# Both MLP products of a decoder layer by Strassen's scheme with seven block products

## The chip, the cores and the metric

The kernel runs on one core of one Trainium2 chip. The metric is the device time of one execution in microseconds, as the median of several runs. A core has five engines with a queue of instructions each: PE multiplies matrices (its results go to PSUM, in banks of 128 partitions x 512 numbers, where a further matmul can add to what stands there), DVE, ACT and POOL work element by element, and SP here issues all DMA transfers. They wait for each other through semaphores alone.

## The reference

The layer is a token mixer (two kinds of attention with gates, an output projection and a layer norm), which the change leaves alone up to that norm, and then an MLP of squared ReLU. Everything is float32; there are 1,024 tokens, the model's width is 1,024 and the hidden width 4,096.

```python
x = _layer_norm(DEEPNORM_ALPHA * x + mix_out, ln1_gain[l], ln1_bias[l])
h = jnp.square(jax.nn.relu(jnp.einsum('bsd,df->bsf', x, w_ff1[l])))
ff_out = jnp.einsum('bsf,fd->bsd', h, w_ff2[l])
x = _layer_norm(DEEPNORM_ALPHA * x + ff_out, ln2_gain[l], ln2_bias[l])
```

## The kernel before

The whole kernel multiplies float32 matrices in three terms. Each operand is split into a high part (the number rounded to the type fp32r) and a low part (number minus high part), and the product is high x high + high x low + low x high: three matmuls of 128x128 weights on 512 columns for what one would do at lower precision. A high part is one copy of the tile, a low part one subtraction.

The norm before the MLP goes by blocks `tb` of 128 tokens: `project_out(tb)` on PE (48 matmuls), `layer_norm1(tb)` on DVE, `turn_x1(tb)` on PE (8 transposes of the normed rows into the bank pair `p_proj`), then ACT copies the high part out of that bank (`x1_high`) and DVE subtracts to get the low part (`x1_low`). PE is one block ahead: `turn_x1(tb)` is followed by `project_out(tb + 2)`. ACT also keeps alpha times the normed rows in SBUF (`keep`, tile `res`), as the start of the second residual sum.

The MLP goes by 16 chunks `c` of 256 hidden features. `up(c)` computes a chunk: 4 banks (two halves of the tokens, two blocks of features), 8 blocks of the inner dimension and 3 terms, 96 matmuls. ACT and DVE turn each bank into squared ReLU and split it into high and low (`hidden`, `hidden_low`). `down(c)` multiplies the chunk by 256 rows of `w_ff2` for all 8 token blocks and both halves of the output, 96 matmuls in 16 groups, and DVE adds each of the 16 banks to `res` (`add_rows`, line 1639). Weights arrive by SP (`load_up`, `load_down`, one load a 512 KB tile, double buffered); DVE makes their high parts (lines 1607, 1613), POOL their low parts (lines 1799, 1804). So the MLP has 16 x 96 x 2 = 3,072 matmuls, all of the same shape. The last two chunks of `down` are computed together, block after block of tokens, and each block's layer norm follows on DVE (lines 1688, 1548 to 1566); ACT scales the rows, POOL adds the bias, SP stores.

The order on each engine is written out by hand. Loops (`Fori`) repeat a body with counting semaphores. PE's program around the MLP reads:

```python
            up(0, 0, True)
            down(0, 0)
            up(1, 1)
            down(1, 1)
            with pe.Fori(1, FC // 2 - 1) as j:
```

Of the kernel before, what the change touches and what calls it, by code (L numbers as in the profile page):

```python
# [168 lines left out]
def layer_kernel(nc, x, w_in, w_branch_a, w_branch_b, w_out, lambda_q1, lambda_k1, lambda_q2,  # L169
                 lambda_k2, subln_gain, ln1_gain, ln1_bias, w_ff1, w_ff2, ln2_gain, ln2_bias,  # L170
                 consts, rope, out):
    with ExitStack() as ctx:
# [79 lines left out]
        w2_l = [at(f"w2_l{t}", 20 + 8 * t, [P, D], F32R) for t in range(2)]
        w1_raw = [at(f"w1_raw{t}", 168 + 4 * t, [P, KT, P]) for t in range(2)]
        w2_raw = [at(f"w2_raw{t}", 176 + 4 * t, [P, D]) for t in range(2)]
        rows_out = at("rows_out", 64, [P, TB, D])
        w1_last_h, w1_last_l = (at(f"w1_last_{i}", 192 + 4 * i, [P, KT, P], F32R) for i in range(2))
        w2_last_h = [at(f"w2_last_h{t}", 168 + 4 * t, [P, D], F32R) for t in range(2)]
        w2_last_l = [at(f"w2_last_l{t}", 176 + 4 * t, [P, D], F32R) for t in range(2)]
# [1585 lines left out]
```

## Time and profile before

| | |
|---|---|
| median of 3 runs | 1628.64 us (1626.85 to 1629.61) |
| the profiled execution, its own time | 1625.79 us |
| its span, first to last instruction | 1623.9 us |
| PE busy | 1560.0 us (96%) |
| DVE busy | 980.0 us (60%) |
| ACT, POOL busy | 493.3 us (30%), 464.3 us (29%) |
| granted clock of PE, mean | 0.989 |
| first matmul of the MLP, last matmul | 911.07 us, 1610.28 us |

Busy times of PE are modelled, so a matmul's row is longer than its share of a dense stream: what a matmul costs is the distance between starts. The span is the time from the first to the last instruction; the execution's own time is 1.9 us longer. Times in rows are microseconds from the start of the span.

### The profile page before, as it was taken

How to read it: one execution, taken by the hardware profiler on the slowest of the kernel's cores; microseconds unless marked ns; L12 is line 12 of the kernel's file. 1: busy time of each engine (PE TensorE's matmuls, PEld its weight loads, DVE VectorE, ACT ScalarE, POOL GpSimd, SP SyncE). 2: the span in 40 equal slices, each digit the busy share in tenths (PEclk: the TensorE clock that was granted, in tenths of full speed). 3: DMA queues.
4: the chain of work that ended last, by engine and by line, in shares of the span. 5: the costliest groups of instructions: out<-in, count | busy, mean ns of one | idle time of the engine just before them, and what ended most of it. 6: DMA issues, size and time to landing. Idle time of an engine off the chain costs nothing.

```text
span 1623.9 us, 20971 instructions
## 1 busy us (share of the span) xinstructions
PE 1560.0 (96%) x7472; PEld 1291.9 (80%) x7472; DVE 980.0 (60%) x1536; ACT 493.3 (30%) x898; POOL 464.3 (29%) x264
## 2 busy tenths in 40 slices
PE   8999999999989888899999999999999999999996
PEld 6788888878867777787878888888888888888885
DVE  3787878878786776843467644444444444434548
ACT  2454555555555554420222211110111111111111
POOL 2544444444332222102300222222122222212322
PEclk9999999999999999999999999999999999999998
DMA  4111112121110000203521311111111111111102
GB/s 165 53 35 58 52 53 77 39 65 30 50 52 20 21 26 13 65 14 117 182 91 52 117 52 52 52 46 34 51 52 52 52 52 38 39 52 52 52 1 104
DMA packets 98669, 92.44 MB, mean 57 GB/s; under 512 B 3632, under 2 KB 85552, under 8 KB 98480
## 3 DMA queue, kind: packets, MB, share of 16 engines
q1 hardware_dynamic: 98608, 91.63, 17.4%
q8 instruction: 38, 0.62, 0.2%
q14 instruction: 23, 0.19, 0.0%
HBM read 81.13 MB, written 10.49 MB: 56 GB/s over the span
## 4 chain that ended last, share of the span: by engine, by line
PE 76%; DVE 9%; issue 9%; POOL 3%; DMA 2%; ACT 1%; SPq 0%; POOLq 0%; DVEq 0%; ACTq 0%
PE p_z L889 6%; PE p_z L888 6%; PE p_z L887 6%; PE p_proj L541 6%; PE p_proj L545 6%; PE p_proj L543 6%; PE p_proj L865 3%; PE p_proj L866 3%; PE p_proj L867 3%; PE p_tr L640 2%; PE p_av L654 2%; PE p_z L808 2%; PE p_z L810 2%; PE p_z L809 2%; PE p_av L867 2%
## 5 line engine op out<-in xcount | busy, mean ns | idle before, releaser
L541 PE MATMUL p_proj<-xt_h,w_hi 128*128 128x512 f32 x640 | 255.4, 399 | 0.8 <-DVE xt_l L1245 0.8
L545 PE MATMUL p_proj<-xt_h,w_lo 128*128 128x512 f32 x640 | 255.0, 398 | 0.0
L543 PE MATMUL p_proj<-xt_l,w_hi 128*128 128x512 f32 x640 | 252.5, 395 | 0.0
L1639 DVE TENSOR_TENSOR res<-p_z,res 128x512 f32<-128x512 f32 x224 | 150.8, 688 | 109.8 <-PE p_z L889 109.8
L1710 POOL TENSOR_TENSOR w_lo<-w_raw,w_hi 128x1024 fp32r<-128x1024 f32 x48 | 120.9, 2520 | 249.0 <-DVE w_hi L1252 248.5
L1799 POOL TENSOR_TENSOR w_l<-w_raw,w_h 128x1024 fp32r<-128x1024 f32 x31 | 79.5, 2585 | 364.5 <-DVE w_h L1607 364.5
L887 PE MATMUL p_z<-w_h,h_h 128*128 128x512 f32 x448 | 174.3, 389 | 0.0
L888 PE MATMUL p_z<-w_l,h_h 128*128 128x512 f32 x448 | 174.3, 389 | 0.0
L889 PE MATMUL p_z<-w_h,h_l 128*128 128x512 f32 x448 | 174.3, 389 | 0.0
L1216 ACT ACTIVATE relu<-p_proj 128x512 f32<-128x512 f32 x30 | 18.0, 599 | 406.7 <-PE p_proj L867 406.7
L545 PEld LDWEIGHTS p_proj<-xt_h,w_lo 128*128 128x128 f32 x640 | 121.5, 190 | 24.1
L541 PEld LDWEIGHTS p_proj<-xt_h,w_hi 128*128 128x128 f32 x640 | 121.3, 189 | 23.1 <-issue 0.8
L543 PEld LDWEIGHTS p_proj<-xt_l,w_hi 128*128 128x128 f32 x640 | 121.3, 190 | 21.6
L1804 POOL TENSOR_TENSOR w_l<-w_raw,w_h 128x1024 fp32r<-128x1024 f32 x30 | 77.9, 2615 | 210.8 <-DVE w_h L1613 210.8
L888 PEld LDWEIGHTS p_z<-w_l,h_h 128*128 128x128 f32 x448 | 84.1, 188 | 17.5
L887 PEld LDWEIGHTS p_z<-w_h,h_h 128*128 128x128 f32 x448 | 84.1, 188 | 17.5
L889 PEld LDWEIGHTS p_z<-w_h,h_l 128*128 128x128 f32 x448 | 84.1, 188 | 17.5
L865 PE MATMUL p_proj<-x1t_h,w_h 128*128 128x512 f32 x232 | 90.4, 390 | 0.4 <-POOL w_l L1799 0.4
L866 PE MATMUL p_proj<-x1t_l,w_h 128*128 128x512 f32 x232 | 90.3, 389 | 0.0
L867 PE MATMUL p_proj<-x1t_h,w_l 128*128 128x512 f32 x232 | 90.2, 389 | 0.0
L1620 DVE SCALAR_TENSOR_TENSOR h_f<-p_proj,relu 128x512 f32<-128x512 f32 x30 | 20.8, 692 | 106.8 <-ACT relu L1216 106.8
L1089 ACT ACTIVATE a_t<-p_tr 128x384 fp32r<-128x384 f32 (+3 forms) x96 | 47.2, 492 | 124.5 <-PE p_tr L640 124.4
(274 smaller groups left out, 3258.2 us busy)
## 6 DMA issues: line engine op xcount, KB each, us to landing
w_raw<-w_ff SPq DMA_DIRECT2D x64, 512.0 KB, 4.0
w_raw<-w_in SPq DMA_DIRECT2D x40, 512.0 KB, 3.8
gate_rows<-gst SPq DMA_DIRECT2D x12, 512.0 KB, 4.9
y<-x SPq DMA_DIRECT2D x8, 512.0 KB, 9.2
wo_raw<-w_out SPq DMA_DIRECT2D x8, 512.0 KB, 8.7
rows<-x SPq DMA_DIRECT2D x8, 512.0 KB, 3.3
out<-rows_out SPq DMA_DIRECT2D x8, 512.0 KB, 2.6
gst<-gate_rows SPq DMA_DIRECT2D x6, 512.0 KB, 4.2
```

The source lines that it names most:

```text
L541: pe.matmul(o, w_hi[n_slot][:, k, :], xt_h[:, k, cols], start=(k == 0), stop=False)
L543: pe.matmul(o, w_hi[n_slot][:, k, :], xt_l[:, k, cols], start=False, stop=False)
L545: mm = pe.matmul(o, w_lo[n_slot][:, k, :], xt_h[:, k, cols], start=False, stop=(k == KT - 1))
L865: pe.matmul(o, w_h[:, k, :], x1t_h[:, k, cols], start=(k == 0), stop=False)
L866: pe.matmul(o, w_h[:, k, :], x1t_l[:, k, cols], start=False, stop=False)
L867: mm = pe.matmul(o, w_l[:, k, :], x1t_h[:, k, cols], start=False, stop=(k == KT - 1))
L887: pe.matmul(o, h_h[par][t][:, rws], w2_h[t][:, cols], start=(t == 0), stop=False)
L888: pe.matmul(o, h_h[par][t][:, rws], w2_l[t][:, cols], start=False, stop=False)
L889: mm = pe.matmul(o, h_l[par][t][:, rws], w2_h[t][:, cols], start=False, stop=(t == 1))
L1639: dve.tensor_tensor(o, by_block(dn_banks[n % 4]), o, ALU.add).then_inc(dn_added, 1)
L1710: pool.tensor_tensor(w_lo[slot][:, :, :], w_raw[:, :, :], w_hi[slot][:, :, :].bitcast(F32), ALU.subtract).then_inc(wt_lo, 1)
L1799: pool.tensor_tensor(low[:, :, :], w1_raw[t][:, :, :], high[:, :, :].bitcast(F32), ALU.subtract).then_inc(w1_lo, 1)
```

## The change

Both MLP products are computed by 2x2 blocks with seven block products in place of eight, in Winograd's form of Strassen's scheme: operands are first added and subtracted blockwise (S1 to S4 of one operand, T1 to T4 of the other), and the seven products P1 to P7 are added up into the four blocks of the result through the sums U2 and U3. Each product is still made of the three terms of high and low parts.

- **Up.** 8 iterations `n` (`ITERS`) of 512 hidden features. A product is 2 groups `t` x 4 inner blocks x 3 terms = 24 matmuls, in the order `UP = (1, 6, 5, 7, 2, 4, 3)` (the first iteration `UP_FIRST`). P1 goes into bank pair A (`p_z[0]`), ACT copies it out (`copy_p1`), and P2 is added on top in the bank. P6 goes into pair B (`p_z[1]`), DVE reads it (`take_u2`: U2 = B + P1), P7 is added on top, DVE reads it again (`take_u3`), P4 is added, and DVE reads it a third time (`take_c21`). P5 and then P3 go into pair C (`p_proj`). Squared ReLU is two ACT passes. ACT makes the high parts of the seven weight operands (`a_high`), DVE the low parts (`a_low`), and DVE the four weight sums (`weights_s1` to `s4`).
- **Between.** The hidden blocks and their four sums (`hidden_s1` to `s4`, DVE) go to HBM scratch, `h_terms`, 7 tiles of 512 KB in each iteration, as do the normed rows (`x1_rows`); `keep` is gone.
- **Down.** 7 products in the order `DOWN = (1, 6, 2, 7, 5, 4, 3)`, each of 8 steps, so 56 steps `g`. A step is 24 matmuls (2 x 4 x 3) on 8 banks, X (`p_z`) and Y (`p_proj`, `p_tr`, `p_av`). SP loads a step's hidden tile `f_a` and its weight tile (`t2c` in product 1, `f_b` in the others but P7, and `f_c` besides in P6), each double buffered by the step's parity; ACT makes two high parts (`step_high`), DVE the weight sums and two low parts (`step_low`), into a ring of four sets. In P6 DVE has two sums in each step. Between products the banks are read in mid-sum (`after_p6` and so on). In the last four steps the order is by rows `j`, and the norms follow (`after_p4`, `after_p3`).
- **The x blocks.** The odd token blocks are combined with the even ones: `x_low` has two sums and three low parts for an odd block, `x_high` four copies for an even and three for an odd one, and POOL makes two sums and two low parts for each pair (`sums`). POOL also prepares most of the first iteration's weights, five operations of 128x1024 between `a_low(1)` and `a_low(6)`, and makes no low parts after that. `turn_x1(TB - 2)` stands in the middle of the last `project_out`.

The diff, cut to its core:

```diff
+UP = (1, 6, 5, 7, 2, 4, 3)
+UP_FIRST = (1, 2, 6, 5, 7, 4, 3)
+DOWN = (1, 6, 2, 7, 5, 4, 3)
+ITERS = FF // 512
+STEPS = 7 * ITERS
...
+            def load_step(g):
+
+                q, it = g // ITERS, g % ITERS
+                m = DOWN[q]
...
+                else:
+                    sp.wait_ge(d_lo, 2 * g - 3)
+                sp.wait_ge(s_h[m], 16 * (it + 1))
+                sp.dma_start(f_a[g % 2][:, :, :].rearrange("p t c -> p (t c)"), h_terms[m][it]).then_inc(da_in[g % 2], 16)
...
+                else:
+                    sp.wait_ge(d_lo, 2 * g - 2)
+                half, col = {6: (1, 1), 2: (1, 0), 5: (1, 1), 4: (1, 0), 3: (1, 1)}[m]
+                sp.dma_start(f_b[g % 2][:, :, :], w2_v[it, half, col]).then_inc(db_in[g % 2], 16)
+                if m == 6:
+                    sp.wait_ge(up_done, UP_END[2, ITERS - 1])
+                    sp.dma_start(f_c[g % 2][:, :, :], w2_v[it, 0, 1]).then_inc(dc_in[g % 2], 16)
...
+            load_step(5)
+            store_hidden(6, last)
+            store_hidden(3, last)
+            for g in range(6, STEPS):
+                load_step(g)
+                if g == 7:
+                    for m in UP:
+                        sp.wait_ge(s_h[m], 16 * ITERS)
+                if 7 <= g < 15:
+                    j = (g - 7) % 4
+                    row, tb = (row_even[j], 2 * j) if g < 11 else (row_odd[j], 2 * j + 1)
+                    sp.dma_start(row[:, :], x1_rows[tb]).then_inc(s_rows, 16)
...
+            def up(n, m):
+
+                wait_up(n, m)
+                for t in range(2):
...
+                    for k in range(4):
...
+                        pe.matmul(o, ah[m][:, k, cols], x_row(m, 0, k), start=fresh and k == 0, stop=False,
+                                  skip_group_check=not fresh)
+                        pe.matmul(o, ah[m][:, k, cols], x_row(m, 1, k), start=False, stop=False,
+                                  skip_group_check=not fresh)
+                        mm = pe.matmul(o, al[m][:, k, cols], x_row(m, 0, k), start=False, stop=k == 3,
+                                       skip_group_check=not fresh)
...
-            up(0, 0, True)
-            down(0, 0)
-            up(1, 1)
-            down(1, 1)
...
+            for n in range(ITERS):
+                for m in UP if n else UP_FIRST:
+                    up(n, m)
...
+            def step_sums(g):
+
+                q, it = g // ITERS, g % ITERS
+                if q == 1:
...
+                    minus(t3c[it], f_b[g % 2], f_c[g % 2]).then_inc(d_sum, 1)
+                    dve.wait_ge(d_sum, 2 * it + 1)
+                    dve.wait_ge(d_lo, 2 * it + 2)
+                    add(t2c[it], t3c[it], t2c[it]).then_inc(d_sum, 1)
...
+            for j in range(4):
+                after_p4(j)
+            for j in range(4):
+                after_p3(j)
```

**PE, the way into the MLP.** In the kernel before, PE ends the last `project_out` (lines 808 to 810), turns block 6 (line 822) and starts `up(0)` (line 865); `p_z1` is the bank pair of the projection:

```order
L808 MATMUL p_z1<-wo_h_91,m_h1_101 128x512
L809 MATMUL p_z1<-wo_l_92,m_h1_101 128x512
L810 MATMUL p_z1<-wo_h_91,m_l1_103 128x512
L834 REGISTER_ALU
L834 COMPARE_AND_BRANCH
L822 MATMUL p_proj<-small_86,rows0_104 128x128 [waits x1_lo,x1_ready]
L822 MATMUL p_proj<-small_86,rows0_104 128x128 x3
L822 MATMUL p_proj<-small_86,rows0_104 128x128 [waits x1_lo]
L822 MATMUL p_proj<-small_86,rows0_104 128x128 x3
L865 MATMUL p_z0<-x1t_h_94,w1_h0_114 128x512 [waits x1_lo,o_read,w1_lo]
L866 MATMUL p_z0<-x1t_l_95,w1_h0_114 128x512
```

In the changed kernel the same four rows of transposes (line 1015) stand among the matmuls of that projection (lines 995 to 997), with 12 of them still to come:

```order
L995 MATMUL p_z1<-wo_h_91,m_h1_99 128x512
L996 MATMUL p_z1<-wo_l_92,m_h1_99 128x512
L997 MATMUL p_z1<-wo_h_91,m_l1_101 128x512
L1015 MATMUL p_proj<-small_86,rows0_102 128x128 [waits t12_ready,x1_ready]
L1015 MATMUL p_proj<-small_86,rows0_102 128x128 x3
L1015 MATMUL p_proj<-small_86,rows0_102 128x128 [waits x1_lo,t12_ready]
L1015 MATMUL p_proj<-small_86,rows0_102 128x128 x3
L995 MATMUL p_z1<-wo_h_91,m_h1_99 128x512
L996 MATMUL p_z1<-wo_l_92,m_h1_99 128x512
L997 MATMUL p_z1<-wo_h_91,m_l1_101 128x512
```

What moved is the wait for the normed block 6 (`x1_ready`): it is 12 matmuls earlier, with those matmuls behind it.

**SP, weights before.** In the kernel before, the loop over chunks issues four weight loads in each chunk, behind waits for the low parts that free the tiles:

```order
L490 ISA [waits w1_lo]
L490 DMA w1_raw0_122<-w_ff1 128x8x128
L490 ISA [waits w1_lo]
L490 DMA w1_raw1_123<-w_ff1 128x8x128
L495 ISA [waits w2_lo]
L495 DMA w2_raw0_124<-w_ff2 128x1024
L495 ISA [waits w2_lo]
L495 DMA w2_raw1_125<-w_ff2 128x1024
```

**SP, between up and down.** In the changed kernel this is SP's order from step 3 to step 6; `f_a0` and `f_a1` are the hidden tiles of even and odd steps, `t2c` the weights, and the stores of `h_terms` are those of the last iteration:

```order
L623 DMA f_a1_179<-h_terms1 128x1024 [waits s_h1,d_lo]
L629 DMA t2c3_187<-w_ff2 128x2x512 [waits d_lo,up_done]
L623 DMA f_a0_178<-h_terms1 128x1024 [waits s_h1,d_lo]
L629 DMA t2c4_188<-w_ff2 128x2x512 [waits d_lo,up_done]
L609 DMA h_terms5<-s1h_144 128x1024 [waits h_sum]
L609 DMA h_terms7<-s3h_145 128x1024 [waits h_sum]
L623 DMA f_a1_179<-h_terms1 128x1024 [waits s_h1,d_lo]
L629 DMA t2c5_189<-w_ff2 128x2x512 [waits d_lo,up_done]
L609 DMA h_terms6<-c11_140 128x1024 [waits h_sum]
L609 DMA h_terms3<-c21_141 128x1024 [waits h_sum]
L623 DMA f_a0_178<-h_terms1 128x1024 [waits s_h1,d_lo]
L629 DMA t2c6_190<-w_ff2 128x2x512 [waits d_lo,up_done]
```

The loads of step 6 (`f_a0`, `t2c6`) stand behind the stores of `h_terms6` and `h_terms3`, which wait for DVE's last two hidden sums (`h_sum`).

**DVE at the same place.** These are the low parts of step 4 to step 6 (line 1539, names with `d_al` and `d_bl`) and the four hidden sums (lines 1926 and 1929):

```order
L1539 TENSOR_TENSOR d_al64_147<-f_a0_178,d_ah64_146 128x1024 [waits d_hi]
L1539 TENSOR_TENSOR d_bl64_149<-t2c4_188,d_bh64_148 128x1024 [waits d_hi]
L1926 TENSOR_TENSOR s1h_144<-c12_142,c22_143 128x1024 [waits s_h5,sq_done22,sq_done12]
L1929 TENSOR_TENSOR s3h_145<-c11_140,c12_142 128x1024 [waits s_h7,sq_done11]
L1539 TENSOR_TENSOR d_al80_163<-f_a1_179,d_ah80_162 128x1024 [waits d_hi]
L1539 TENSOR_TENSOR d_bl80_165<-t2c5_189,d_bh80_164 128x1024 [waits d_hi]
L1929 TENSOR_TENSOR c11_140<-s1h_144,c11_140 128x1024 [waits s_h1,h_sum]
L1929 TENSOR_TENSOR c21_141<-c21_141,c11_140 128x1024 [waits s_h2,sq_done21,h_sum]
L1539 TENSOR_TENSOR d_al96_155<-f_a0_178,d_ah96_154 128x1024 [waits d_hi]
L1539 TENSOR_TENSOR d_bl96_157<-t2c6_190,d_bh96_156 128x1024 [waits d_hi]
```

The sums for terms 6 and 3, the third and fourth, stand behind the low parts of step 5.

**SP in P6.** Two steps of the eight, each with `f_a`, `f_b`, `f_c` and a tile of normed rows:

```order
L705 DMA row_even2_209<-x1_rows 128x1024
L623 DMA f_a0_178<-h_terms6 128x1024 [waits s_h6,d_lo]
L639 DMA f_b0_180<-w_ff2 128x2x512 [waits d_lo]
L642 DMA f_c0_182<-w_ff2 128x2x512 [waits up_done]
L705 DMA row_even3_210<-x1_rows 128x1024
L623 DMA f_a1_179<-h_terms6 128x1024 [waits s_h6,d_lo]
L639 DMA f_b1_181<-w_ff2 128x2x512 [waits d_lo]
L642 DMA f_c1_183<-w_ff2 128x2x512 [waits up_done]
```

**DVE in P6.** One step (two sums, two low parts) and the start of the next:

```order
L1929 TENSOR_TENSOR t3c2_194<-f_b0_180,f_c0_182 128x1024 [waits dc_in0,db_in0]
L1926 TENSOR_TENSOR t2c2_186<-t3c2_194,t2c2_186 128x1024 [waits d_lo,d_sum]
L1539 TENSOR_TENSOR d_al96_155<-f_a0_178,d_ah96_154 128x1024 [waits d_hi]
L1539 TENSOR_TENSOR d_bl96_157<-t2c2_186,d_bh96_156 128x1024 [waits d_hi]
L1929 TENSOR_TENSOR t3c3_195<-f_b1_181,f_c1_183 128x1024 [waits dc_in1,db_in1]
L1926 TENSOR_TENSOR t2c3_187<-t3c3_195,t2c3_187 128x1024 [waits d_lo,d_sum]
```

In the kernel before nothing like it stands on DVE; what is new is that a step's first DVE operation waits for two loads whose buffers the step before last must have freed (`d_lo`).

## Rows read from the trace of the kernel before

**Rows 1.** The page: span, part 1 (busy us of each engine), HBM traffic of part 3.

```profile
span 1623.9 us, 20971 instructions
...
PE 1560.0 (96%) x7472; PEld 1291.9 (80%) x7472; DVE 980.0 (60%) x1536; ACT 493.3 (30%) x898; POOL 464.3 (29%) x264
...
HBM read 81.13 MB, written 10.49 MB: 56 GB/s over the span
```

**Rows 2.** Windows: busy us per engine, granted clock, DMA share, GB/s.

```profile
core 0: us, PE busy (x) PEld busy (x) DVE busy (x) ACT busy (x) POOL busy (x), PEclk, DMA share, GB/s
1000.00:1100.00 100.00, 100.00 (x442) 82.78 (x442) 41.26 (x63) 11.71 (x20) 25.68 (x10) 1.00 0.16 53
...
1580.00:1624.00 44.00, 30.67 (x136) 25.07 (x134) 39.51 (x86) 8.05 (x13) 14.33 (x6) 0.90 0.24 96
```

**Rows 3.** The page, part 5: one of the costliest groups.

```profile
L887 PE MATMUL p_z<-w_h,h_h 128*128 128x512 f32 x448 | 174.3, 389 | 0.0
```

**Rows 4.** Waits of PE from 820 us to the end.

```profile
PE p_z L865 <- DVE x1t_l L1245: 1.1, 1, 1.1
PE p_proj L865 <- POOL w_l L1799: 0.4, 1, 0.4
```

**Rows 5.** PE in order of time: MLP's first matmul and its last.

```profile
start us, us, engine line op out<-in xcount [idle before <-releaser]
911.07 0.47 PE L865 MATMUL p_z<-x1t_h,w_h 128*128 128x512 f32 x1
...
1610.28 0.39 PE L928 MATMUL p_av<-w_last_h,h_l 128*128 128x512 f32 x1
```

**Rows 6.** Timeline around a norm of 128 tokens, PE, ACT and DVE.

```profile
898.50 1.03 PE L822 MATMUL p_proj<-small,rows 128*128 128x128 f32 x8
...
888.38 1.06 ACT L1157 ACTIVATE m_h<-res 128x1024 fp32r x1
...
899.21 1.09 ACT L1175 ACTIVATE x1t_h<-p_proj 128x512 f32 x2 [2.49 <-PE p_proj L822]
...
895.41 1.22 DVE L1245 TENSOR_TENSOR m_l<-res,m_h 128x1024 fp32r<-128x1024 f32 x1
...
899.96 1.29 DVE L1245 TENSOR_TENSOR x1t_l<-p_proj,x1t_h 128x512 f32 x2 [3.33 <-ACT x1t_h L1175]
...
901.17 1.28 DVE L1575 SCALAR_TENSOR_TENSOR rows<-rows,p_z 128x512 f32<-128x512 f32 x2
...
906.01 1.28 DVE L1566 SCALAR_TENSOR_TENSOR rows<-rows,vecs,gains 128x1024 f32<-128x1024 f32 x1
```

**Rows 7.** Tile wo_raw: POOL and DVE on it together, landing of its loads.

```profile
L1793 POOL TENSOR_TENSOR wo_l<-wo_raw,wo_h x4: 2406/2663/3371, 794.6 to 812.0; 128x1024 fp32r<-128x1024 f32 x4
L1245 DVE TENSOR_TENSOR wo_l<-wo_raw,wo_h x4: 1216/2310/3426, 806.4 to 813.1; 128x1024 fp32r<-128x1024 f32 x4
...
DMA to landing us min/median/max: 6.3/8.7/10.9
```

**Rows 8.** Windows with the busiest queue, and one kind of load.

```profile
740.00:745.00 5.00, 5.00 (x24) 4.14 (x23) 0.00 (x0) 0.00 (x0) 0.00 (x0) 1.00 0.88 299
...
790.00:795.00 5.00, 4.53 (x21) 3.44 (x20) 4.10 (x4) 2.27 (x3) 2.77 (x2) 1.00 1.06 392
...
w_raw<-w_ff SPq DMA_DIRECT2D x64, 512.0 KB, 4.0
```

**Rows 9.** DVE in order of time, the last two norms.

```profile
1607.78 1.28 DVE L1688 TENSOR_TENSOR rows_out<-p_proj,res 128x512 f32<-128x512 f32 x2
...
1610.61 2.17 DVE L1554 SCALAR_TENSOR_TENSOR rows_out<-rows_out,vecs,gains 128x1024 f32<-128x1024 f32 x1
...
1614.72 0.68 DVE L1688 TENSOR_TENSOR rows_out<-p_tr,res 128x512 f32<-128x512 f32 x1
...
1619.57 1.28 DVE L1566 SCALAR_TENSOR_TENSOR rows_out<-rows_out,vecs,gains 128x1024 f32<-128x1024 f32 x1
```

More of the change, by code:

```diff
@@ L252, in layer_kernel @@
[L252 to L258, printed above, removed]
@@ new lines, in layer_kernel @@
+        SETS = {set_at(g) for g in range(STEPS)}
+        d_ops = {o: [at(f"d_{n}{o}", o + 4 * i, [P, 2, NH], F32R) for i, n in enumerate(("ah", "al", "bh", "bl"))]
+                 for o in SETS}
+        f_a = [at(f"f_a{i}", 32 + 4 * i, [P, 2, NH]) for i in range(2)]
+        f_b = [at(f"f_b{i}", 40 + 4 * i, [P, 2, NH]) for i in range(2)]
+        f_c = [at(f"f_c{i}", 168 + 4 * i, [P, 2, NH]) for i in range(2)]
+        t2c = [at(f"t2c{i}", (8 + 4 * i) % 32, [P, 2, NH]) for i in range(ITERS)]
@@ L933, in _ @@
+            for g in range(STEPS - 4):
+                down(g)
+            for j in range(4):
+                for g in range(STEPS - 4, STEPS):
+                    if j == 0:
+                        wait_step(g)
+                    for t in range(2):
+                        mm = down_part(g, t, j, False, g == STEPS - 1 and t == 1)
+                mm.then_inc(dn_last, 1)
         @block.scalar
@@ L1187, in _ @@
             split_merged(1, 1)
[L1189 to L1198 removed]
+            for tb in range(TB - 2):
+                split_merged(tb + 2, tb % 2)
+                norm(tb, tb % 2)
+                if tb % 2 == 0 and tb:
+                    sums_high(tb // 2 - 1)
+                x_high(tb)
@@ L1236, in _ @@
-            for s in range(2):
-                norm(2 * TB - 2 + s, s)
+            for t in range(2):
+                if t == 0:
+                    act.wait_ge(up_done, 1)
+                    act.wait_ge(o_done, 2 * TB)
+                else:
+                    act.wait_ge(up_done, UP_END[1, 0])
+                act.activation(p1[:, t, :], up_bank(1, t), ACT.Copy).then_inc(p1_read, 1)
+            for m in (7, 5, 6):
+                a_high(m, 0)
+            x_high(TB - 1)
+            sums_high(3)
@@ new lines, in _ @@
+            for g in range(4, STEPS):
+                step_high(g)
+                if ITERS + 3 <= g < ITERS + 7:
+                    j = g - ITERS - 3
+                    if j == 0:
+                        act.wait_ge(dn_done, ITERS)
+                    act.activation(p1d[:, j, :], dn_banks[j], ACT.Copy).then_inc(p1_copied, 1)
+            for q in range(TB):
+                norm(TB + q, q % 2)
+                if q < TB - 1:
+                    act.wait_ge(ln_scale, q + 1)
+                    row = row_odd[q] if q < 4 else row_even[q - 4]
+                    act.activation(row[:, :], row[:, :], ACT.Copy, scale=ln_r[q % 2]).then_inc(ln_scaled, 1)
@@ L1699, in _ @@
+            for j in range(4):
+                after_p4(j)
+            for j in range(4):
+                after_p3(j)
         @block.gpsimd
```

994 lines of the change are left out of this document (659 added, 335 removed).

## The prediction

> **What bounds the kernel now.** I read the page first: PE is busy for 1560.0 of 1623.9 us, DVE for 980.0, and HBM traffic is 56 GB/s [rows 1]. The windows show where the average hides something: in the MLP PE is busy for 100.00 of 100 us at full clock, while DVE has 41, ACT 12 and POOL 26, and only in the last 44 us does PE fall to 30.67 with DVE at 39.51 [rows 2]. The waits of PE behind 820 us are two, 1.1 and 0.4 us [rows 4]. So the MLP is bound by the number of matmuls, and its end by DVE.
>
> What a matmul costs is read from starts, since the 389 ns of its row [rows 3] overlap the next. The MLP's first matmul starts at 911.07 and its last at 1610.28 [rows 5]: 699.2 us, less 1.5 of waits [rows 4] and 1.0 for the eight transposes that stand in between [rows 6], is 696.7 us for 3,071 distances, 0.227 us each. The window agrees: 442 matmuls in 100 us [rows 2].
>
> **1. Fewer matmuls: -87.1 us.** Up has 8 iterations x 7 products x 24, down 56 steps x 24: 2,688 in place of 3,072. 384 x 0.227 = 87.1. Form and types are the same. A product or a step is then 24 x 0.227 = 5.44 us, an iteration of up 38.1 us.
>
> **2. The way into the MLP: +4.0 us.** Before, DVE waits 3.3 us for ACT's high part, makes two low parts from 899.96 and starts the next norm at 901.17; the transposes are at 898.50 [rows 6]. For block 5 it now has two sums (0.6 us each by these rows, from 899.2), waits for a copy by ACT (0.6), and has three low parts: 899.2 + 1.3 + 0.7 + 2.0 = 903.2, 2.0 us later. The normed block 6, ready at 906.01 + 1.28 = 907.3 before [rows 6], comes at 909.3. Before, its transposes ended just ahead of 911.07 [rows 5] and began 1.0 us earlier, at 910.1; now they are 12 matmuls (2.7 us) earlier, so PE asks at 907.5 and waits 1.8, and up begins at 909.3 + 1.0 + 2.7 = 913.0: +2.0 us. Then POOL's chain: ACT has four copies of 0.6 from 910.0 and one of 1.06 [rows 6], to about 913.6; POOL makes a low part and three sums, ACT a copy (1.1), POOL the low part that P6 waits for. By the median of 2.66 us [rows 7] that is 913.6 + 10.6 + 1.1 + 2.7 = 928.0, and PE arrives after two products and a turn at 913.0 + 10.9 + 1.0 = 924.9. It waits 3.1 us. Where POOL and DVE worked together, single operations took up to 3.37 us on POOL and 3.43 on DVE in place of 2.41 and 1.22 [rows 7], so I take 3.5. With the 1.5 us of old waits gone: 2.0 + 3.5 - 1.5 = 4.0. At 2.41 us for POOL and no wait at the turn it is 0, at 3.37 us for all it is 8.
>
> **3. Up in its steady state: 0.** An iteration gives DVE 20 operations on 128x1024 (seven low parts, four weight sums, five reads of banks, four hidden sums): 1.22 us from SBUF, 1.27 for two halves of a bank pair [rows 6], 25 of 38.1 us. ACT has 16 at 1.06 [rows 6], 17 us. The reads in mid-sum cover themselves: U2 is read when P6 ends, and P7, the next on that pair, comes one product (5.44 us) later, against 1.3 us of reading; DVE has at that point just finished two sums and a low part at about 10.3 us of the iteration and P6 ends at 10.9. U3 and C22 are read at 23 and 24.3, wanted at 27.2 and 32.6; A has 10.9 us until the next P1. Were a read late by more than 4 us, PE would wait 8 times. Loads and stores are 11 tiles (5.8 MB) in 38.1 us, 151 GB/s against the 392 that the queue has carried [rows 8].
>
> **4. From up to down: +3.8 us.** Let 0 be the start of the last iteration; up ends at 38.1, step 6 is due at 38.1 + 6 x 5.44 = 70.7. The sets are a ring of four, so step 6 may be made early, but its loads stand behind the stores of hidden terms 6 and 3. The chain, at 1.25 us on DVE and 1.06 on ACT: the hidden copies of step 3 land near 42, its low parts end at 45, the last bank is read at 46.3, squared at 48.5; step 4's copies and low parts end at 52.0, the first two hidden sums at 54.5; behind their stores go step 5's loads at 55.0 to 55.5. A single 512 KB load lands after 4.0 us, and the queue moves 392 GB/s [rows 8], so 1.34 us a tile and 2.7 us besides; step 5's land near 60.5, its low parts end at 63, the last hidden sums at 65.3. Then two stores and two loads: 65.3 + 3 x 1.34 + 2.7 = 72.0, a copy and a low part, 74.5. PE waits 3.8 us. Lower bound 0 (if every link saves 0.5 us); upper 6.5, with the 8.7 us to landing of eight loads in flight [rows 7] in place of 6.7. Step 7's loads are issued right behind, it is ready 2.5 us later and due 5.4 later: no second wait.
>
> **5. The eight steps of P6: +2 us.** A step moves f_a, f_b, f_c and, in seven of them, a tile of rows: 4 x 0.524 = 2.1 MB per 5.44 us, 386 GB/s. The best window shows 392 [rows 8], so it just fits. The tighter limit is the loop through two buffers: low part of step g - 2, loads (about 6.2 us to the last of three: 2.7 + 2.5 x 1.34), two sums, copy, low part (2.5 + 1.1 + 1.25 + 0.3 = 5.1). That is 11.3 us for two steps, 5.65 each against 5.44: 0.2 x 8 = 1.7, and nothing is left of the ring after item 4. I take 2. DVE's four operations are 5.0 us a step, also just inside.
>
> **6. The rest of down: 0.** Two loads, two or three DVE operations and two copies a step: (6 + 3.6) / 2 = 4.8 us at most. The bank reads come at the fourth to seventh step, with a product in between.
>
> **7. The end: +0.7 us.** Before, DVE's norms set it: 6.9 us from 1607.78 to 1614.72 for the first of the last two, which scales the rows itself, and from the last matmul's end (1610.28 + 0.23) to DVE's (1619.57 + 1.28) it is 10.3 us [rows 5, 9]. Now four norms of odd rows follow the low parts of step 55 (ready some 20 us before PE ends) and take 4.6 us each, since the bank read and the statistics of one half are done; the even four queue behind them, so DVE ends 11 us behind PE. It is 0 if DVE keeps up, 3 if it starts late.
>
> **Sum.** -87.1 + 4.0 + 3.8 + 2.0 + 0.7 = -76.6. The profiled execution took 1625.8 (its span 1623.9 and 1.9 around it), 2.8 below the median of the runs, so 1549.2 by its measure and 1552.0 as a median.
>
> **Rivals.**
> - *The loads bind P6* (chance 0.22). For: 386 of 392 GB/s, and with eight loads in flight a tile took 8.7 us to land at the median, 10.9 at most [rows 7]. With these the loop is 6.9 or 8.0 us a step, 12 or 20 us in place of 2: 1562 to 1570. Against: only three or four tiles are in flight here. Plain bandwidth could be the limit too: at the 299 GB/s of the other busy window [rows 8] a step's 2.1 MB take 7.0 us, 11 us more over the seven steps, 1561; of the 0.22 this has 0.07. The Trainium skill (DMA: Bandwidth & Descriptors, Specifications) gives about 358 GB/s as HBM's limit for a core: an estimate by it is 5.86 us a step, 3 us more than PE over seven steps. By that rule, the trace does not agree, with 392 GB/s over 5 us [rows 8].
> - *Everything is hidden* (0.13): the links of item 4 are each shorter and POOL is not slowed. 1542 to 1546.
> - *Slower than before* (0.03). The mechanism would be the two-buffer loop of down. To eat 76.6 us over 56 steps it must take 6.8 us a step in all products, landings of 10 us where 4.0 is the row; in P6 alone, 15 us a step. DVE's idle share in the MLP [rows 2] speaks against it.
> - *The matmuls get slower* (0.05). P3 and P4 of up, 384 matmuls, read their 512 columns in four pieces of 128, and no row shows such a read. At half as long again it is +44 us, 1596. To undo the gain all 2,688 would have to take 0.255 us.
>
> **The numbers.** Chances: forecast with its own range 1546 to 1559, 0.57; the rest as above. The range is 1543 to 1568. A measurement tells about 0.2% (3.3 us) from no change: faster 0.96, same 0.01, slower 0.03.
>
> **What would show it.** 2,688 matmuls at 0.227 us between up's first and down's last; one wait of PE of 1 to 2 us at line 1015 and one of 2 to 6 at the first P6, on POOL; no wait in iterations 1 to 7; one at step 6, on DVE's low part; then small ones or none in steps 8 to 15. Waits in each iteration of up, or in products behind P6, would make me wrong; so would a distance of matmuls other than 0.227 us.

## The result, and the profile after

The changed kernel takes 1584.67 us (median of 4 runs, 1582.09 to 1588.35) where the kernel before takes 1628.38 beside it (4 runs, 1626.85 to 1629.61): a ratio of 0.9734, with a 95% interval of 0.9709 to 0.9758, 43.7 us less. I had forecast 76.6 less, and 1543 to 1568 us as the range. The direction was right, the size was not.

The page of the changed kernel, the rows that answer to [rows 1]:

```profile
span 1580.4 us, 19531 instructions
...
PE 1482.8 (94%) x7088; PEld 1225.7 (78%) x7088; DVE 1100.3 (70%) x1448; ACT 667.0 (42%) x1028; POOL 344.4 (22%) x224
```

PE is 77 us less busy than before, near the 87 of the forecast. The span is only 43.5 shorter. So the matmuls are gone, and PE now waits. The waits of PE from 820 us to the end, to be read against [rows 4] (total us, times, longest):

```profile
PE p_proj L1015 <- DVE rows L1862: 14.0, 4, 6.9
PE p_z L1072 <- DVE c L1926: 7.9, 1, 7.9
PE p_z L1094 <- DVE d_bl L1539: 4.4, 1, 4.4
PE p_proj L1094 <- DVE d_bl L1539: 1.9, 2, 1.0
```

It was 1.5 us in two waits, now it is 28.2 in eight. The third row's 4.4 and the fourth row's 1.9 were forecast as 3.8 and 2. The first two rows were not. PE in order of time shows where they stand: the first matmul of up, the first of down and the last, the answer to [rows 5]:

```profile
926.79 0.39 PE L1072 MATMUL p_z<-x_h,a_h 128*128 128x512 f32 x1
...
1245.34 0.39 PE L1094 MATMUL p_z<-d_bh,d_ah 128*128 128x512 f32 x1
...
1559.66 0.39 PE L1096 MATMUL p_z<-d_bh,d_al 128*128 128x512 f32 x1
```

These three starts place the whole loss in four stretches. Each stretch is of the profiled execution, "forecast" is by the terms of the prediction:

| stretch | before | forecast | measured | missed by |
|---|---|---|---|---|
| start of the span to up's first matmul | 911.1 | 913.1 | 926.8 | 13.7 |
| to down's first (1,344 matmuls) | | 309.3 | 318.6 | 9.2 |
| to the last matmul (1,344 matmuls) | | 310.6 | 314.3 | 3.7 |
| last matmul to the end of the span | 13.6 | 14.3 | 20.7 | 6.4 |

The four add up to 33.0 us, and the span missed its forecast by 33.1 (43.5 in place of 76.6). The second forecast is 1,344 x 0.2268 us (87.1 / 384), 1.0 for eight transposes and 3.5 for the wait that I had put at the first P6; the third has the waits of 3.8 and 2.0.

Windows of PE (busy us, matmuls, granted clock, DMA share, GB/s):

```profile
core 0: us, PE busy (x), PEclk, DMA share, GB/s
890.00:900.00 10.00, 8.56 (x35) 0.83 0.31 107
920.00:930.00 10.00, 9.02 (x35) 0.73 0.13 52
960.00:970.00 10.00, 4.00 (x10) 0.66 0.16 52
1000.00:1200.00 200.00, 200.00 (x884) 1.00 0.41 147
1280.00:1290.00 10.00, 7.44 (x23) 0.66 1.01 386
```

In the steady part PE is never idle, and 884 matmuls start in 200 us as in the 442 of 100 us before [rows 2]: the distance of 0.227 us holds, also for P3 and P4 with their rows read in four pieces. The other windows show a second price of a wait. Behind the long ones the granted clock is at half (1.2 GHz) for some microseconds, 0.66 and 0.73 in the mean of 10 us, and matmuls come every 0.43 us (923.60, 924.03, 924.46 in the order of time) in place of 0.227. By the starts of matmuls this took 2.3 us more behind the wait that ended at 1282.56 (eleven starts in 4.81 us, to 1287.37, where 2.50 is the steady time).

Now the first stretch. A timeline of POOL, DVE and PE around the norm of block 6, the answer to the last row of [rows 6]; L1856 and L1861 work on 128x1 numbers, L1862 is the norm's last step:

```profile
914.90 1.42 POOL L2264 TENSOR_TENSOR x_l<-b_f,x_h 128x512 fp32r<-128x512 f32 x1 [4.87 <-ACT x_h L1387]
...
915.30 1.04 DVE L1856 SCALAR_TENSOR_TENSOR vecs<-vecs 128x1 f32<-128x1 f32 x1
916.28 1.26 POOL L2264 TENSOR_TENSOR res_r<-b_f,res_r 128x512 fp32r<-128x512 f32 x1
...
916.57 0.99 DVE L1861 TENSOR_TENSOR vecs<-vecs 128x1 f32<-128x1 f32 x1
917.50 2.34 POOL L2269 TENSOR_TENSOR a_l<-r,a_h 128x1024 fp32r<-128x1024 f32 x1
917.60 3.33 DVE L1862 SCALAR_TENSOR_TENSOR rows<-rows,vecs,gains 128x1024 f32<-128x1024 f32 x1
...
920.98 1.97 PE L1015 MATMUL p_proj<-small,rows 128*128 128x128 f32 x8 [6.89 <-DVE rows L1862]
```

L1862 took 1.28 us before [rows 6] and takes 3.33; L1856 takes 0.22 us where POOL is idle and here 1.04. Look at the ends: POOL's three operations end at 916.32, 917.54 and 919.84; DVE's end at 916.34, at 917.56, and at 920.93, 1.09 behind POOL's, little less than the operation alone. In these rows a DVE operation that began beside one of POOL's ended behind it, by at most its own time. 25 us later a DVE operation that reads one input from a bank runs beside POOL unharmed, in its usual 0.68 us:

```profile
942.34 1.75 POOL L2264 TENSOR_TENSOR x_l<-b_f,x_h 128x512 fp32r<-128x512 f32 x1
...
942.86 0.68 DVE L1539 TENSOR_TENSOR res_r<-p_proj,res_r 128x512 fp32r<-128x512 f32 x1
```

That is what the Trainium skill states (SBUF — State Buffer, Who interferes with whom): VectorE's second SBUF input and GpSimd share a port pair, the one that issues first holds it for its whole instruction, and a VectorE instruction with at most one SBUF input, outside its two-port modes, doesn't contend. The trace agrees in each of these rows.

The second stretch: POOL's last weight sum of iteration 0 (it stands behind POOL's low part for P6 and the sums and low parts of the last pair of blocks), a low part of DVE's beside it, the load of iteration 1's `r11`, DVE's first weight sum of that iteration, DVE's read of bank pair B (`take_u3`) and the matmul of P4 that overwrites it:

```profile
946.29 3.37 POOL L2288 TENSOR_TENSOR r<-r,r 128x1024 f32<-128x1024 f32 x1
...
947.33 3.41 DVE L1539 TENSOR_TENSOR a_l<-r,a_h 128x1024 fp32r<-128x1024 f32 x1
...
951.24 0.46 SPq L570 DMA_DIRECT2D r<-w_ff  x1
...
956.15 1.22 DVE L1929 TENSOR_TENSOR r_s<-r,r 128x1024 f32<-128x1024 f32 x1 [3.14 <-DMA r<-w_ff]
...
964.63 1.22 DVE L1926 TENSOR_TENSOR c<-p_z,p 128x1024 f32<-128x1024 f32 x1
...
966.00 0.77 PE L1072 MATMUL p_z<-res_r,a_h 128*128 128x512 f32 x1 [7.94 <-DVE c L1926]
```

P7 had ended at 958.06. But `take_u3` stands on DVE behind iteration 1's weights, whose load was issued at 951.24 only: SP's queue stood behind that low part, which took 3.41 us beside POOL and ended at 950.74. The load waits for POOL's sum too, which ended at 949.66, so the low part alone held it for 1.1 us. DVE idled 3.14 us for the load, then worked off the weights, and read the bank 6.6 us after it was ready.

At step 6 of down, the stores of SP, DVE's low part and PE's wait:

```profile
1272.08 1.58 SPq L609 DMA_DIRECT2D h_terms<-c  x2
...
1280.01 1.23 DVE L1539 TENSOR_TENSOR d_al<-f_a,d_ah 128x1024 fp32r<-128x1024 f32 x1 [6.69 <-ACT d_ah L1441]
...
1282.56 0.80 PE L1094 MATMUL p_z<-d_bh,d_ah 128*128 128x512 f32 x1 [4.42 <-DVE d_bl L1539]
```

In P6, DVE's sum of `f_b` and `f_c` in its eight steps (min/median/max ns, first and last start), and the landing of `f_c`:

```profile
L1929 DVE TENSOR_TENSOR t3c<-f_b,f_c x8: 1225/1226/1227, 1289.0 to 1331.8; 128x1024 f32<-128x1024 f32 x8
...
DMA to landing us min/median/max: 6.0/7.1/9.2
```

Eight starts from 1289.0 to 1331.8 are 6.1 us a step, where I had 5.65.

At the end, POOL's bias for one row and DVE's first large operation of the next norm (L1850):

```profile
1539.22 2.40 POOL L2293 TENSOR_TENSOR row_odd<-row_odd,gains 128x1024 f32<-128x1024 f32 x1 [589.57 <-ACT row_odd L1531]
...
1539.64 3.06 DVE L1850 SCALAR_TENSOR_TENSOR row_odd<-row_odd,vecs,gains 128x1024 f32<-128x1024 f32 x1
```

3.06 us, in place of 1.28 for the same operation of the first norm (1535.97), when POOL was idle. It is the same lock: POOL ends at 1541.62, DVE 1.08 later.

### The profile page after: what moved, and what is told of

Same layout as the page of the kernel before. It is cut to its first block, busy times and chain, and to the rows that moved or that the text cites. A ratio compares the mean times of both kernels' runs of the same rounds, so it can differ in the third digit from the quotient of the medians.

```text
span 1580.4 us, 19531 instructions
## 1 busy us (share of the span) xinstructions
PE 1482.8 (94%) x7088; PEld 1225.7 (78%) x7088; DVE 1100.3 (70%) x1448; ACT 667.0 (42%) x1028; POOL 344.4 (22%) x224
## 4 chain that ended last, share of the span: by engine, by line
PE 64%; DVE 14%; issue 10%; DMA 6%; POOL 3%; ACT 2%; SPq 1%; POOLq 0%; DVEq 0%; ACTq 0%
PE p_proj L726 6%; PE p_proj L730 6%; PE p_proj L728 6%; PE p_z L1072 4%; PE p_z L1076 4%; PE p_z L1074 4%; PE p_tr L825 2%; DMA f_c<-w_ff 2%; PE p_av L839 2%; PE p_z L1096 2%; PE p_z L1094 2%; PE p_z L1095 2%; PE p_proj L1072 2%; PE p_proj L1074 2%; PE p_proj L1076 2%
## 5 line engine op out<-in xcount | busy, mean ns | idle before, releaser
L1539 DVE TENSOR_TENSOR d_al<-f_a,d_ah 128x1024 fp32r<-128x1024 f32 x56 | 68.5, 1224 | 88.2 <-ACT d_ah L1441 87.9
L1441 ACT ACTIVATE d_ah<-f_a 128x1024 fp32r<-128x1024 f32 x56 | 59.2, 1058 | 144.0 <-PE p_av L1096 54.9
L1094 PE MATMUL p_z<-d_bh,d_ah 128*128 128x512 f32 x256 | 100.7, 393 | 4.4 <-DVE d_bl L1539 4.4
L1095 PE MATMUL p_z<-d_bl,d_ah 128*128 128x512 f32 x256 | 100.4, 392 | 0.0
L1096 PE MATMUL p_z<-d_bh,d_al 128*128 128x512 f32 x256 | 100.3, 392 | 0.0
L1072 PE MATMUL p_z<-x_h,a_h 128*128 128x512 f32 x256 | 99.7, 389 | 0.0
L1076 PE MATMUL p_z<-x_h,a_l 128*128 128x512 f32 x256 | 99.6, 389 | 0.0
L1074 PE MATMUL p_z<-x_l,a_h 128*128 128x512 f32 x256 | 99.6, 389 | 0.0
L1539 DVE TENSOR_TENSOR a_l<-r,a_h 128x1024 fp32r<-128x1024 f32 x45 | 57.5, 1280 | 45.2 <-ACT a_h L1401 45.2
L761 PE MATMUL p_z<-k_hi,q_st 128*128 128x512 f32 (+2 forms) x192 | 68.2, 359 | 10.1 <-ACT e L1247 8.7
```

Source lines behind the costliest of these rows:

```text
L761: pe.matmul(z[:, lo:lo + w], lhs, k_hi[m][:, lo:lo + w], start=True, stop=False)
L1072: pe.matmul(o, ah[m][:, k, cols], x_row(m, 0, k), start=fresh and k == 0, stop=False, skip_group_check=not fresh)
L1074: pe.matmul(o, ah[m][:, k, cols], x_row(m, 1, k), start=False, stop=False, skip_group_check=not fresh)
L1076: mm = pe.matmul(o, al[m][:, k, cols], x_row(m, 0, k), start=False, stop=k == 3, skip_group_check=not fresh)
L1094: pe.matmul(o, a_h[:, t, rws], b_h[:, t, :], start=first, stop=False, skip_group_check=more)
L1095: pe.matmul(o, a_h[:, t, rws], b_l[:, t, :], start=False, stop=False, skip_group_check=more)
```

## The experiments

The theories, after the trace. **A:** POOL's sums and low parts hold DVE up in the norms, and this makes the 13.7 us. **B:** the transposes inside the last projection do, since PE asks 12 matmuls earlier. For the other stretches: the order of DVE in iteration 0, the order of loads and stores before step 6, the tiles of rows that share the queue with P6, and POOL in the last norms. The stretches of all kernels, each of one profiled execution, in us:

| kernel | time | up's first matmul | up | down | end |
|---|---|---|---|---|---|
| changed kernel | 1584.67 | 926.8 | 318.6 | 314.3 | 20.7 |
| e1, turn after the projection | 1586.21 (1 run) | 925.1 | 321.8 | 316.1 | 21.7 |
| e2, POOL almost idle in the norms | 1571.38 (1 run) | 913.5 | 321.1 | 314.6 | 20.6 |
| e3, sums on DVE | 1573.97 | 916.1 | 320.4 | 316.0 | 20.9 |
| e4, bank reads first | 1577.35 | 928.1 | 311.8 | 316.7 | 20.8 |
| e5, loads before stores | 1578.85 (1 run) | 929.8 | 318.6 | 307.9 | 21.0 |
| e6, last norms without POOL | 1579.36 | 927.9 | 318.4 | 313.9 | 17.6 |
| e7, rows after P6 | 1578.64 (1 run) | 925.6 | 318.5 | 311.7 | 21.2 |
| e8, e3 to e7 together | 1560.42 | 913.8 | 317.1 | 304.4 | 17.3 |

Where nothing ahead of up differs (the changed kernel, e4 to e7), its first matmul lies between 925.6 and 929.8: differences under 4 us in that column say nothing. Where nothing in down differs (the changed kernel, e1 to e4, e6), down takes 313.9 to 316.7 us and PE's waits in P6 are 1.8 to 3.6 us, so differences of that size say nothing either. The kernel before had 1626.77 beside e1 to e4 (7 runs) and 1627.07 beside e5 to e8 (9 runs).

**e1, the turn after the projection (B).**

```diff
-            project_out(TB - 1, 1, lambda: turn_x1(TB - 2, 0))
+            project_out(TB - 1, 1)
+            turn_x1(TB - 2, 0)
```

> The changed kernel with the transposes of block 6 behind the last project_out, as in the kernel before, not in its middle. There PE waited 6.9 us for the normed rows of block 6, which DVE finished at 920.9. Theory A (DVE is slowed by POOL's work in the norm stage, so the block is late): the wait stays, shorter by the 12 matmuls (2.7 us) that now stand ahead of it, about 4 us, and up's first matmul is within 1 us of the changed kernel's 926.8. Rival B (the place of the transposes is what costs): the wait goes to under 1 us and up starts near 921.

The turn of block 6:

```profile
921.96 1.97 PE L1015 MATMUL p_proj<-small,rows 128*128 128x128 f32 x8 [4.25 <-DVE rows L1863]
```

The wait falls from 6.89 to 4.25, by the 12 matmuls now ahead of it, but one of 1.14 follows at up's first matmul, and that starts at 925.1: 1.7 us sooner than before the edit, inside the scatter, though I had expected it within 1 us. PE waits for the same norm in another place. B falls.

**e2, POOL almost idle in the norms (A).** POOL's sums run on 4 of 512 columns for the first three pairs of blocks, and ACT writes copies in place of POOL's low parts, so most of these sums and low parts is left out, and ACT has two copies more in each of these pairs.

```diff
+                c = slice(0, 1) if j < 3 else slice(0, P)
-                pool.tensor_tensor(b11_f[:, :, :], t2_f[:, :, :], b11_f[:, :, :], ALU.subtract).then_inc(t34_ready, 1)
+                pool.tensor_tensor(b11_f[:, :, c], t2_f[:, :, c], b11_f[:, :, c], ALU.subtract).then_inc(t34_ready, 1)
...
+                if j < 3:
+                    act.activation(x_block(7, 1, j), b11_f[:, :, :], ACT.Copy).then_inc(t34_lo, 1)
```

> POOL's part in the first three pairs of token blocks is left out: its two sums are done on 4 of 512 columns, and ACT writes the two low parts as copies in place of POOL's subtractions (so T3, T4 and their low parts are not the right numbers for 6 of the 8 blocks). DVE's own work is unchanged. Theory A (POOL slows DVE): the pair of low parts of an odd block takes 1.3 us in place of 2.9, the small operations 0.2 in place of 1.06, the waits of 2.2, 2.2 and 6.9 us at the turns fall to 0, 0 and about 2, and up starts some 11 us earlier, near 916. Rival C (DVE's own added work in odd blocks sets it): the waits stay within 1 us of theirs and up starts at 925 or later.

Waits of PE from 820 us, the two greatest, and the same DVE operations of block 6's norm as above:

```profile
PE p_z L1072 <- DVE c L1930: 6.4, 1, 6.4
PE p_proj L1015 <- DVE rows L1866: 5.9, 2, 4.4
```

```profile
907.83 0.22 DVE L1860 SCALAR_TENSOR_TENSOR vecs<-vecs 128x1 f32<-128x1 f32 x1
...
908.46 1.29 DVE L1866 SCALAR_TENSOR_TENSOR rows<-rows,vecs,gains 128x1024 f32<-128x1024 f32 x1
```

0.22 and 1.29 us in place of 1.04 and 3.33. Of the four waits at turns two are gone, block 6's is 1.57, and up begins at 913.5, 13.3 us sooner. The 4.4 is at the turn of block 7, where POOL's weight sums still stand beside the norm. A is shown: POOL's place beside the norms costs the first stretch, not the number of DVE's operations.

**e3, the same work with the sums on DVE.** Nothing is left out: DVE makes POOL's two sums and two low parts of each pair.

```diff
+                dve.tensor_tensor(b11_f[:, :, :], t2_f[:, :, :], b11_f[:, :, :], ALU.subtract).then_inc(t34_ready, 1)
+                dve.tensor_tensor(b21_f[:, :, :], b21_f[:, :, :], t2_f[:, :, :], ALU.subtract).then_inc(t34_ready, 1)
...
+            def low34(j):
+                for i, (m, f) in enumerate(((7, b11_f), (4, b21_f))):
...
+                    sub(x_block(m, 1, j), f[:, :, :], x_block(m, 0, j)).then_inc(t34_lo, 1)
...
-            for j in range(3):
-                sums(j)
```

> The same work as the changed kernel, but the two sums and two low parts of each pair of token blocks run on DVE, not POOL, for all four pairs: 16 operations of about 0.6 us more on DVE, all of that work gone from POOL. Theory A: faster than the changed kernel by 8 to 14 us (1571 to 1577), up starting near 917, since POOL cost DVE more than the work itself is worth; the first iteration's wait of 7.9 us gets shorter too, because POOL's last weight sum comes about 8 us earlier. Rival C (DVE's own work binds): slower than the changed kernel by about 5 us.

1573.97 us (4 runs, 1570.87 to 1576.18), ratio 0.9666 (0.9646 to 0.9686). Up begins at 916.1: with four more operations a pair DVE is quicker than with POOL's help. The wait of 7.9 us in iteration 0 is 4.0 here, but up as a whole is no shorter (320.4), as the wait at the turn of block 7 grew from 2.7 to 4.9 and half clock stands behind both. What is left of the trouble is the norm of block 7, beside POOL's weight chain:

```profile
916.82 2.40 POOL L2271 TENSOR_TENSOR a_l<-r,a_h 128x1024 fp32r<-128x1024 f32 x1 [3.73 <-ACT a_h L1401]
917.03 1.28 DVE L1844 BATCH_NORM_STATS2 vecs<-rows 128x6 f32<-128x512 f32 x2
...
919.18 3.38 POOL L2277 TENSOR_TENSOR r_s<-r,r 128x1024 f32<-128x1024 f32 x1
...
920.41 2.16 DVE L1856 SCALAR_TENSOR_TENSOR vecs<-vecs 128x1 f32<-128x1 f32 x1
...
928.63 1.76 PE L1015 MATMUL p_proj<-small,rows 128*128 128x128 f32 x7 [4.85 <-DVE rows L1862]
```

Two more lines of the rule in one place: the statistics (one SBUF input, two at 0.64) run beside POOL undisturbed, and the 128x1 operation, 0.22 alone, ends at 922.57 with POOL's 3.38 us operation. The wait at this turn is 4.85.

**e4, bank reads first in iteration 0.**

```diff
+                    take_u3(0)
+                    take_c22(0)
                     weights_s3(1)
                     weights_s1(1)
                     a_low(1, 1)
```

> The changed kernel with one move on DVE in the first iteration of up: the reads of U3 and C22 stand ahead of the four weight sums and low parts for iteration 1. In the changed kernel P7 of iteration 0 ends at 958.1, but DVE waits for weights by DMA until 956.2 and reads U3 only at 964.6, behind seven operations, and PE waits 7.9 us for it. Theory D (the order on DVE behind a late load): the wait falls to about 1.5 us, the stretch at half clock behind it goes, and the time is 7 to 10 us less (1575 to 1578). Rival E (PE would wait next for the weights of iteration 1): the wait moves to the first product of iteration 1 and the time is within 3 us of the changed kernel's.

1577.35 us (4 runs, 1573.40 to 1578.98), ratio 0.9683 (0.9664 to 0.9701). The waits inside up:

```profile
PE p_z L1072 <- DVE c L1926: 1.4, 1, 1.4
PE p_z L1072 <- DVE u L1926: 1.3, 1, 1.3
```

The 7.9 became 1.4, a new one of 1.3 stands at the read of U2 in iteration 1, since DVE now does the weights later, and up is 6.8 us shorter. So the order on DVE made the wait, with the late load behind it.

**e5, loads before stores.**

```diff
+            load_step(5)
             store_hidden(5, last)
             store_hidden(7, last)
-            load_step(5)
+            load_step(6)
             store_hidden(6, last)
             store_hidden(3, last)
```

> The changed kernel with one move on SP: the loads of step 5 ahead of the stores of hidden terms 5 and 7, the loads of step 6 ahead of the stores of terms 6 and 3. In the changed kernel PE waits 4.4 us for step 6, as forecast from the place of its loads. Theory F (the place of the loads): the wait at step 6 is gone, and with it a stretch at half clock; the first and last matmul of down are 5 to 7 us less apart than 314.4 us. Rival G (the bandwidth that stores and loads share): the wait is still over 2 us.

1578.85 us in one run. PE's only waits in down are these:

```profile
PE p_proj L1095 <- DVE d_bl L1540: 2.9, 2, 1.7
```

The 4.4 at step 6 is gone, and down is 6.4 us shorter: 4.4 of wait and 2.3 at half clock behind it are gone (the window of 1280 to 1290 us, at 0.66 in the changed kernel, is at 1.00 here), and PE waits 1.0 more in P6 (2.9 in place of 1.9). The 0.7 left over is not placed. The 2.9 lies inside the 1.8 to 3.6 of the kernels whose down is the same, so these runs don't show that it comes from PE's arriving sooner.

**e6, last norms without POOL.** DVE scales each row and adds its bias in one operation, as the last norm did already; ACT's and POOL's parts go.

```diff
-                layer_norm(row_odd[j][:, :], j, j % 2, TB, None, False, st_rows[j]).then_inc(ln_scale, 1)
+                layer_norm(row_odd[j][:, :], j, j % 2, TB, None, True, st_rows[j]).then_inc(f_ready, 1)
...
-                pool.tensor_tensor(row[:, :], row[:, :], gains[:, 1, :], ALU.add).then_inc(f_ready, 1)
```

> The changed kernel with the end of all eight norms on DVE alone (scale and bias in one operation), as it is for the last; ACT's scaling and POOL's bias sums are gone. In the changed kernel the first large operation of a norm takes 3.0 us beside POOL's sum and a norm 5.45. Theory H (POOL slows DVE's norms): that operation takes 1.3 us, a norm 4.9 to 5.1 although it has one large operation more, and DVE ends some 3 to 4 us earlier; total 1580 to 1582. Rival I (the norms start late, their length does not matter): DVE's end moves by less than 1 us.

1579.36 us (4 runs, 1577.95 to 1584.78), ratio 0.9713 (0.969 to 0.9735). The operation that took 3.06:

```profile
1541.50 1.28 DVE L1846 SCALAR_TENSOR_TENSOR row_odd<-row_odd,vecs,gains 128x1024 f32<-128x1024 f32 x1
```

A norm takes 4.98 us (1541.50 to 1546.48 between two of these) in place of 5.45, though DVE has one more operation of 1.28 in each; from the last matmul to the end it is 3.1 us less. Of the time as a whole the runs can't tell it from the changed kernel's: the intervals overlap.

**e7, rows after P6.** The eight tiles of normed rows are loaded in steps 16 to 19, two in each, in place of one in each of steps 7 to 14.

```diff
-                if 7 <= g < 15:
-                    j = (g - 7) % 4
+                for i in range(2 * g - 32, 2 * g - 30) if 16 <= g < 20 else ():
+                    j = i % 4
```

> The changed kernel with the eight tiles of normed rows loaded in steps 16 to 19, not 7 to 14, so that a step of P6 moves 1.57 MB, not 2.1. If bandwidth sets the pace of P6, the last of three loads lands within 6 us and DVE's steps come every 5.3 us or less, and the waits of PE in steps 8 to 15 (1.9 us in the changed kernel) are gone. If the loop through two buffers sets it with loads at their unloaded speed, the waits stay.

1578.64 us in one run. The only wait of PE left in down, and the landing of `f_c`:

```profile
PE p_z L1094 <- DVE d_bl L1539: 4.6, 1, 4.6
```

```profile
DMA to landing us min/median/max: 5.8/6.3/7.6
```

A tile lands in 6.3 us in place of 7.1, DVE's sums come every 5.8 us (1287.5 to 1327.9) in place of 6.1, and no wait is left in P6. In the seven kernels with the fourth tile the median landing is 7.1 to 7.6 us and a step 6.0 to 6.4; in the two without it (this one and e8) they are 6.3 and 6.9, 5.8 and 5.9. A window of P6 in the changed kernel and in this one (granted clock, DMA share, GB/s behind PE's matmuls):

```profile
1300.00:1310.00 10.00, 10.00 (x46) 1.00 0.96 347
```

```profile
1300.00:1310.00 10.00, 10.00 (x46) 1.00 0.79 266
```

The signs that I had set don't all fall on one side. The waits went, as for bandwidth, but a step still takes 5.8 us, where bandwidth as the limit wanted 5.3 or less. With three tiles the DMA engines are not full, at 0.72 to 0.81 from 1290 to 1330 us, which leaves the loop through two buffers to set the step; no run with a third buffer tests that. With four they are busy for 0.96 to 1.01 of the time in each window from 1280 to 1330 us, so there the runs don't separate the loop, with slower landings, from full DMA engines.

**e8, e3 to e7 together.**

The five diffs above in one kernel.

> Five edits together: the sums of token blocks on DVE, U3 read first in iteration 0, the loads of steps 5 and 6 ahead of the stores, norms without POOL, rows loaded behind P6. If the causes are separate, their gains add: 11 us of the first, 7 of the second less the 4 that the first already gives, 5 of the third, 3 of the fourth, 2 of the fifth: 1584 less 24, 1558 to 1562. If they hide each other, 1565 or more.

1560.42 us (5 runs, 1554.27 to 1560.99), ratio 0.9586 (0.957 to 0.9601): 66.7 us less than before, 24 less than the change alone, and the best version here. The parts' gains add up, as expected. The three longest waits of PE (the fourth is 0.9 us), and two windows of PE in down:

```profile
PE p_proj L1016 <- DVE rows L1859: 7.3, 2, 5.2
PE p_z L1073 <- DVE u L1937: 1.7, 1, 1.7
PE p_z L1073 <- DVE c L1937: 1.4, 1, 1.4
```

```profile
1250.00:1530.00 280.00, 280.00 (x1237) 1.00 0.63 217
...
1320.00:1330.00 10.00, 10.00 (x45) 1.00 1.03 406
```

Down has no wait at all: 304.4 us for 1,344 matmuls, 0.227 each. The stretches gained 13.0, 1.4, 9.9 and 3.4 us, 27.7 together; they are of this kernel's fastest run, 1554.27 us, and the medians differ by 24. The 1.4 is small beside e4's 6.8 because the wait at the turn of block 7 is 5.2 us here, where it was 2.7: POOL's weight chain, which all these edits leave on POOL, locks the norm as in e3's rows, and there is half clock behind the wait (the window of 920 to 930 us is at 0.71).

## Why the prediction missed

**Item 1, fewer matmuls, was right.** The steady distance is 0.227 us. With all waits gone in down, 1,344 matmuls take 304.4 us in e8 against 304.8 by the item's price. The rival of slower matmuls falls with it.

**Item 2, the way into the MLP, is the step that failed most: 13.7 of the 33 us.** It priced DVE's norm of block 6 as 2.0 us late. It was 13.6 late: the row that ends it (L1862) starts at 906.01 before [rows 6] and at 917.60 now, and takes 2.05 longer. The turn of block 5 (898.50 before [rows 6]) begins at 904.85, 6.4 us late, mostly by the two waits ahead of it (4.4) and the half clock behind one of them (1.6). From there to the end of the norm it is 16.1 us in place of 8.8: 2.0 more as forecast, and 5.3 more in four places where DVE stands beside POOL (two low parts 2.92 us for 1.29, then 1.04 for 0.22, 0.99 for 0.16, 3.33 for 1.28). I had the lock in my own rows: in [rows 7] POOL takes up to 3371 ns where 2406 is the least, and DVE 3426 for 1216, while both work on the same tile, and in [rows 9] the norm's first large operation (L1554), otherwise 1.28 us as well, takes 2.17. I used that spread for POOL's chain alone, as a risk of some tenths, and never asked which of DVE's norm operations stand beside POOL's new sums. Each norm has four with both inputs in SBUF (L1850, L1856, L1861 and L1862), and each can wait for an operation of POOL. Of the 15.7 us that up starts later, 11.3 are waits at the three turns ahead (2.22, 2.21, 6.89); of the other 4.4, 3.8 are half clock by the starts of matmuls, 1.6 behind the wait of 2.21 and 2.2 behind that of 6.89. The forecast had no term for the clock, although it had waits.

**Item 3, up's steady state, was right where it was checked, and it didn't cover iteration 0.** Iterations 1 to 7 have no wait. The item checked the reads in mid-sum by the order of the steady iteration; in iteration 0 they stand behind the next iteration's weights, whose loads are late (7.94 us; e4). A wait of 2.70 at the turn of block 7, with no half clock behind it, and 1.7 us at half clock behind the 7.94 (966.00 to 969.93) make up most of the rest of that stretch. The wait of 3.5 for POOL at the first P6, which item 2 had, came in no run: also where up begins as early as forecast (913.5 in e2, 913.8 in e8), PE waits before that, at the turn of block 7 (4.4 and 5.2), for a norm that POOL's chain holds up. The chain was there, and I had the wrong wait for it.

**Item 4, up to down, was right:** 4.4 us against 3.8, and e5 shows that the loads behind the stores are the cause. The half clock behind it, 2.3 us by the starts of matmuls, was not in the sum; it is the largest part of the 3.7 that down missed by, with 0.6 for the longer wait. The rest is not placed.

**Item 5, P6, was near in its sum (1.9 against 2), less so in its parts.** The closeness is in part luck: with the same code in down the waits are 1.8 to 3.6 us from kernel to kernel. A step took 6.1 us, not 5.65 (and the terms given for the landing, 2.7 + 2.5 x 1.34, make 6.05, not 6.2). Eight steps at 6.1 us are 5.3 us over PE's own; that PE waited for 1.9 only fits the 2.3 us that it had itself lost at half clock behind step 6, which the sum didn't have. The rival in which loads bind P6 is not ruled out for four tiles a step, since the DMA engines were busy for 0.96 and more of the time there; it cost far less than the 10 to 18 us that it had. A fixed rate of 299 GB/s is ruled out: the queue carried 386 GB/s over 10 us in the changed kernel and 406 in e8, there in steps with two tiles of rows each behind P6 and with no wait. The 358 GB/s of the Trainium skill (DMA: Bandwidth & Descriptors, Specifications) is exceeded in both windows.

**Item 6 was right:** no wait behind P6.

**Item 7, the end, was mis-sized:** 7.1 us against 0.7. DVE began 25.5 us before PE's last matmul (1534.21), which with eight norms of 4.6 us gives the 11 us behind PE that the item had. The eight took 43.0 us (to 1577.24), 5.4 each: 6.2 us more. The first norm, with POOL idle, takes 3.67 us (1535.97 to 1539.64 between two L1850), the next 5.45, so the lock is 1.8 us a norm. e6 shows that POOL's part in this is 3.1 at least, since there DVE does POOL's and ACT's work besides and still ends 3.1 sooner.

The chance of "faster" needed only item 1. What made the range too narrow is that its terms were all waits on a chain that I had followed, with one value each for the durations, and that iteration 0 and the norms were only followed in part.

## What to carry to other kernels

When a change gives work to POOL, list DVE's operations beside it that read both inputs from SBUF, small ones too, and price each as late by up to what is left of POOL's operation; here it was cheaper to give DVE the work itself (e3). Follow the first iteration's order on its own: a steady state without waits says nothing about it. And price a wait of PE at more than its length, by the half clock that can stand behind it: here 2.3 us more behind 4.4, and 1.6 more behind one wait of 2.2.
